# Stick-breaking attention: the sums of later key blocks enter as a high and a low part, and the first values product opens its bank

## The reference, cut to what matters

```
z = einsum('bqhd,bkhd->bhqk', q_b, bk) * HEAD_DIM ** -0.5
causal = kpos[None, :] < qpos[:, None]
log_beta = log_sigmoid(z)
log_one_minus = where(causal, log_sigmoid(-z), 0.0)
tail = cumsum(log_one_minus, reverse=True) - log_one_minus
a = where(causal, exp(log_beta + tail), 0.0)
return einsum('bhqk,bkhd->bqhd', a, bv)
```

## Time and profile before

| | |
|---|---|
| median of 3 runs | 1705.36 us |
| lowest and highest | 1705.3 and 1705.81 us |
| the profiled execution: span from first to last instruction | 1703.1 us |
| its own whole time | not listed apart from the span |
| stick-breaking stage | 955 to 1051 us of the span |

### The profile page before, as it was taken

One profiled execution on the slowest core, in us unless ns is written; L12 is line 12 of the kernel. 1 busy time (PEld: TensorE's weight loads), 2 busy tenths in 40 slices (PEclk: granted clock), 3 DMA queues, 4 the chain that ended last, 5 costly groups with the idle time before them and its releaser, 6 DMA issues.

```text
span 1703.1 us, 23621 instructions
## 1 busy us (share of the span) xinstructions
PE 1694.7 (100%) x8117; PEld 1360.8 (80%) x8117; DVE 877.5 (52%) x1406; ACT 656.0 (39%) x1091; POOL 656.8 (39%) x276
## 2 busy tenths in 40 slices
PE   9999999999999999999999999999999999999998
PEld 7888767788888888888788766778888988888887
DVE  6644875564655551217497675542233775555013
ACT  7333645433222223327524576452223622222122
POOL 2444322344544444435343000224444244444443
PEclk9999999999999999999999999999999999999999
DMA  5345311223333322334322111122333232233231
GB/s 202 118 148 151 102 63 50 75 88 123 99 99 99 98 90 96 99 99 150 114 99 76 50 45 44 50 67 95 99 99 94 88 101 91 97 99 97 101 96 66
DMA packets 47635, 162.29 MB, mean 95 GB/s; under 512 B 5724, under 2 KB 7900, under 8 KB 47304
## 3 DMA queue, kind: packets, MB, share of 16 engines
q1 hardware_dynamic: 43440, 150.70, 27.5%
q10 hardware_dynamic: 4120, 10.59, 1.9%
HBM read 156.91 MB, written 4.76 MB: 95 GB/s over the span
## 4 chain that ended last, share of the span: by engine, by line
PE 52%; issue 32%; POOL 12%; DVE 1%; ACT 1%; DMA 1%; POOLq 0%; SPq 0%; ACTq 0%; DVEq 0%
PE ps L505 14%; PE ps L506 14%; PE ps L507 14%; POOL w_lo L442 12%; PE ps L1131 1%; PE ps L1129 1%; PE ps L1130 1%; PE ps L704 1%; PE ps L686 1%; DMA w_raw<-stream 1%; PE ps L730 1%; PE ps L1030 1%; PE ps L989 1%; PE ps L1011 1%; PE ps L958 1%
## 5 line engine op out<-in xcount | busy, mean ns | idle before, releaser
L442 POOL TENSOR_TENSOR w_lo<-w_raw,w_hi 128x1024 fp32r<-128x1024 f32 x260 | 642.8, 2475 | 1026.2 <-ACT w_hi L1212 999.3
L505 PE MATMUL ps<-u_hi,w_hi 128*128 128x512 f32 x1336 | 539.6, 404 | 0.2 <-ACTq L1802 0.2
L507 PE MATMUL ps<-u_hi,w_lo 128*128 128x512 f32 x1336 | 521.1, 390 | 0.0
L506 PE MATMUL ps<-u_lo,w_hi 128*128 128x512 f32 x1336 | 520.5, 390 | 0.0
L1212 ACT ACTIVATE w_hi<-w_raw 128x1024 fp32r<-128x1024 f32 x271 | 285.4, 1055 | 391.5 <-PE ps L507 326.3
L505 PEld LDWEIGHTS ps<-u_hi,w_hi 128*128 128x128 f32 x1336 | 251.1, 188 | 56.7 <-issue 5.8
L507 PEld LDWEIGHTS ps<-u_hi,w_lo 128*128 128x128 f32 x1336 | 250.8, 188 | 53.4
L506 PEld LDWEIGHTS ps<-u_lo,w_hi 128*128 128x128 f32 x1336 | 251.3, 188 | 50.9 <-issue 1.4
L1635 ACT ACTIVATE tmp<-tmp 128x512 f32<-128x512 f32 x44 | 27.8, 633 | 213.2 <-DVEq L2317 213.2
L2327 DVE TENSOR_TENSOR a_lo<-tmp,a_hi 128x512 f32 (+1 forms) x44 | 104.2, 2368 | 4.7
L505 PE MATMUL ps<-a_hi,w_hi 128*128 (+1 forms) x264 | 102.9, 390 | 0.0
(11 more groups left out here) (410 smaller groups left out, 2434.6 us busy)
## 6 DMA issues: line engine op xcount, KB each, us to landing
w_raw<-stream SPq DMA_DIRECT2D x277, 512.0 KB, 3.5
g_rep<-g_one ACTq DMA_DIRECT2D x1, 2560.0 KB, 12.8
spread<-m_rows ACTq DMA_DIRECT2D x4, 512.0 KB, 4.0
tmp<-tmp ACTq DMA_DIRECT2D x32, 64.0 KB, 2.5
bias<-g_rep ACTq DMA_DIRECT2D x1, 2048.0 KB, 10.1
outT<-hT SPq DMA_DIRECT2D x13, 128.0 KB, 1.8
hT<-xT SPq DMA_DIRECT2D x3, 512.0 KB, 7.5
mem_in<-memT ACTq DMA_DIRECT2D x1, 1024.0 KB, 4.8
```

Of the source, the lines that this page charges most:

```text
L442: pool.tensor_tensor(w_lo[:, slot], w_raw[:, slot], w_hi[:, slot].bitcast(F32), ALU.subtract)\
L505: pe.matmul(out, wh, xh, start=start, stop=False)
L506: pe.matmul(out, wh, xl, start=False, stop=False)
L507: return pe.matmul(out, wl, xh, start=False, stop=stop)
```

## The change

- `negones_r`, a rounded copy of `negones` in its own place, is made by ACT at the start (line 1423 is followed by one more copy).
- The plain fp32 product of line 1011 becomes two fp32r products, `negones_r` times `sums_hi` and times `sums_lo`.
- ACT makes `sums_hi` for both heads of step g-1, at the end of turn g, behind that step's two `sticks`. POOL makes `sums_lo` from it. PE waits for `sums_lo` (`sb_sum_lo`) before the two products.
- The running sums lie in other places: `even_sums` and `odd_sums`. DVE waits, before it overwrites one, until the low part of the sums that lay there has been made.
- The product of zeros goes, with the two memsets on DVE that filled it; the first values product of a pair has `start` set instead.

```diff
+        negones_r = at("negones_r", [P, P], F32R, kept_at + 4 * TAB["negones"])
...
-        sum_tiles = [[tmp[2], tmp[3]], [at("sum2", [P, T], F32, mk_at), at("sum3", [P, T], F32, mk_at + 2 * K)]]
+        sum_at = [arena + 103 * K, mk_at]
+        even_sums = [at(f"even_sums{e}", [P, T - P], F32, sum_at[e]) for e in range(2)]
+        odd_sums = [at(f"odd_sums{e}", [P, T - 2 * P], F32, sum_at[e] + 4 * (T - P)) for e in range(2)]
+        sums_hi = [ar("sums_hi0", [P, T - P], F32R, 72), ar("sums_hi1", [P, T - P], F32R, 78)]
+        sums_lo = [at(f"sums_lo{e}", [P, T - P], F32R, sum_at[e] + 4 * (2 * T - 3 * P)) for e in range(2)]
...
+        def of_sums(h, n):
+
+            return 6 * (h // 2) + 2 * n + h % 2 + 1
...
@@ GpSimd, behind its weight tiles up to BY_VECTOR[0]
+            for h, i in B_STEPS:
+                if i > 0:
+                    n = QT - 1 - i
+                    pool.wait_ge(named("sb_sum_hi"), of_sums(h, n))
+                    pool.tensor_tensor(sums_lo[h % 2][:, 0:T - i * P], sums(h % 2, n, i * P, T),
+                                       sums_hi[h % 2][:, 0:T - i * P].bitcast(F32), ALU.subtract)\
+                        .then_inc(named("sb_sum_lo"), 1)
@@ TensorE
-            pe.wait_ge(named("zeros"), 2)
-            pe.wait_ge(consts, 7)
+            pe.wait_ge(consts, 8)
...
                         if i < QT - 1:
-                            pe.wait_ge(named("sb_acc"), 6 * (h // 2) + 2 * (QT - 2 - i) + e + 1)
-                            m = pe.matmul(ps[:, b, P:w], negones, sums(e, QT - 2 - i, (i + 1) * P, T), start=False,
+                            pe.wait_ge(named("sb_sum_lo"), of_sums(h, QT - 2 - i))
+                            pe.matmul(ps[:, b, P:w], negones_r[:, :], sums_hi[e][:, 0:w - P], start=False,
+                                      stop=False, skip_group_check=True)
+                            m = pe.matmul(ps[:, b, P:w], negones_r[:, :], sums_lo[e][:, 0:w - P], start=False,
                                           stop=True, skip_group_check=True)
...
                     if i == QT - 1:
                         acquire(bo)
-                        pe.matmul(ps[:, bo, :], zero_l[:, :], zero_r[:, :], start=True, stop=False,
-                                  skip_group_check=True)
...
-                                  sticks[(s + e) % 4][:, 0:T - i * P], start=False, stop=e == 1 and i == 0,
+                                  sticks[(s + e) % 4][:, 0:T - i * P], start=i == QT - 1, stop=e == 1 and i == 0,
@@ ScalarE, at the start
             act.activation(negtri_r[:, :], negtri, ACT.Copy).then_inc(consts, 1)
+            act.activation(negones_r[:, :], negones, ACT.Copy).then_inc(consts, 1)
@@ ScalarE, in the stage, behind the two sticks of step g-1
+                    for e in range(2):
+                        h, i = B_STEPS[2 * (g - 1) + e]
+                        if i > 0:
+                            n = QT - 1 - i
+                            act.wait_ge(named("sb_acc"), of_sums(h, n))
+                            act.activation(sums_hi[e][:, 0:T - i * P], sums(e, n, i * P, T), ACT.Copy)\
+                               .then_inc(named("sb_sum_hi"), 1)
@@ VectorE
-            step(dve.memset(zero_l[:, :], 0.0))
-            dve.sem_inc(named("zeros"), 1)
-            step(dve.memset(zero_r[:, :], 0.0))
-            dve.sem_inc(named("zeros"), 1)
...
                         if i > 0:
                             n = QT - 1 - i
+                            if h >= 2 or n == 2:
+                                dve.wait_ge(named("sb_sum_lo"), of_sums(h, n) - (2, 6, 4)[n])
```

More of the change, by code:

```diff
@@ L232, in build @@
         soft_hi = [ar(f"soft_hi{i}", [P, T], F32R, at_kib) for i, at_kib in enumerate((64, 66, 74, 76))]
-        sum_tiles = [[tmp[2], tmp[3]], [at("sum2", [P, T], F32, mk_at), at("sum3", [P, T], F32, mk_at + 2 * K)]]
-        def sums(e, n, c0, c1):
-            x = sum_tiles[e][n % 2]
-            return x[:, c0 - 3 * P:c1 - 3 * P] if n == 0 else x[:, c0:c1]
+        sum_at = [arena + 103 * K, mk_at]
[3 more added lines that the diff above has]
+        sums_lo = [at(f"sums_lo{e}", [P, T - P], F32R, sum_at[e] + 4 * (2 * T - 3 * P)) for e in range(2)]
+        def sums(e, n, c0, c1):
+            first = (QT - 1 - n) * P
+            x = (odd_sums if n % 2 else even_sums)[e]
+            return x[:, c0 - first:c1 - first]
+        def of_sums(h, n):
+            return 6 * (h // 2) + 2 * n + h % 2 + 1
         sticks = [tmp[0], tmp[1], at("stick2", [P, T], F32, mv_at), at("stick3", [P, T], F32, mv_at + 2 * K)]
@@ L257, in build @@
         GATE_BANK = 2
-        zero_l = ar("zero_l", [P, P], BF16, 72)
-        zero_r = ar("zero_r", [P, T], BF16, 73)
         tab_in = ar("tab_in", [P, 2 * P], F32, 96)
@@ L2457, in _ @@
                         j = 2 * g + e
-                        i = B_STEPS[j][1]
+                        h, i = B_STEPS[j]
                         w = T - i * P
```

## The result

The changed kernel takes 1713.9 us (median; 1713.48 to 1714.9) against 1705.49 (1705.3 to 1705.81) for the kernel before on the same chip: ratio 1.005, 95% interval 1.0038 to 1.0062. The profiled execution has a span of 1712.4 us at a granted clock of 0.998.

What follows compares the result with a forecast made beforehand. PE's own order of work was taken as the bound. Lateness at i = 0 of 7.0 us over four pairs, less 0.5 for an earlier S, gave 1705.36 + 6.5 = 1711.9 us; range 1706.0 to 1717.0.

Steps and rivals of the forecast that it cites:

- Off PE, 4.6 us: PE's saving in the stick-breaking stage: 2.5 us at width 384, 1.2 at 256, 0.9 for the zero products.
- PE's own order of work sets the end: In the stick-breaking stage, time taken off PE is won and time PE is made to wait is lost in full.
- The chain from S: From S, a pair's second 384 wide `sticks` start, through ACT, POOL, PE: second head's sums in at S + 4.05.
- Eight waits: PE waiting for POOL's `sums_lo` at the new products' line eight times, longest at width 384 and in the last pair.
- 11 in all: PE's total wait for `sums_lo`, some 11 us, about 2 to 3 us in each pair.
- S itself: Start of the second 384 wide `sticks`: 0 to 0.3 us earlier in each of pairs 2 to 4, -0.5 in all.
- second rival: POOL and DVE hold each other, 0.9 us per pair on the chain: 3.7 us more, 1715.6; 14 in 100.
- The last pair: At i = 0 PE is 2.6 us later, with no next step's z or weight quarter in front of the product.
- three things that the prediction named: POOL much shorter or longer than 1.02 us at 384; waits at i = 1 and 2; clock under 1.00 behind waits.
- A quick POOL: Same chain, but POOL's 384 wide subtraction takes 0.5 us; decides below 0.65: +2.4 us, 1707.8; 16 in 100.
- No wait at i = 0: Low parts are there when PE wants them at width 384, so PE keeps its 4.6 us: 1700.8; 8 in 100.
- The other edits at nothing: DVE's new wait was covered by idle time, the weight tile's high part made early, the extra copy and memsets nothing.

Runs made afterwards that it cites:

- products_alone: Changed kernel without the splitting of the sums on ACT and POOL; the two fp32r products read the step's own softplus parts: 1701.65 us, ratio 0.9978.
- middle_split: Kernel before with the split at width 256 alone, on ACT and POOL as in the change, and no zero product: 1705.64 us, ratio 1.0002.
- middle_on_pool: Kernel before with the split at width 256 alone, both halves on POOL, and no zero product: 1705.48 us, ratio 1.0.
- hi_only: Changed kernel without POOL's subtraction; one product, `negones_r` times `sums_hi`, in place of two: 1706.08 us, ratio 1.0005.
- blanks: Changed kernel with fifteen unread 512 wide bf16 products on PE in the last pair's waits for `soft_lo` and `sums_lo`: 1712.95 us, ratio 1.0044.
- pool_twice: Changed kernel with each low part subtracted twice on POOL, PE waiting for the second: 1732.42 us, ratio 1.016.
- hi_on_pool: Changed kernel with both halves of the split on POOL and no copies for the sums on ACT: 1707.37 us, ratio 1.0013.

## Why the prediction was right, and where by its own steps it was not

The forecast was 1711.9 us; 1713.9 came, by the chain that it named.

- **Off PE, 4.6 us.** The widths cost what was counted: 0.17 us for a 384 wide fp32r product, two of width 256 some 0.23 (0.15 saved was counted, 0.19 would be right). With no sums to wait for, 3.7 us of the sum are won (`products_alone`). "PE's own order of work sets the end" held in full in the pairs 2 and 3, where 1.16 us a pair are won and PE never stands still; in pairs 1 and 4 a second chain, DVE's and ACT's, is close enough behind to keep some 0.5 us each. With POOL at work that chain is 0.5 us later in pairs 2 to 4 (`middle_split`, `middle_on_pool`), for which the sum has no term.
- **The chain from S.** Copies at S + 0.68, as counted; 0.47 each for 0.52; POOL starts at S + 1.28 for 1.34; 0.98 us for 1.02 at width 384. The first head's low part is there at S + 2.27 for 2.36, the second's at S + 3.25 for 3.38. Behind them the hand-over and the weight load were oversized: 0.05 and 0.11 us (the product holds PE for 0.28 instead of 0.17) where 0.14 and 0.19 were counted. The second head's sums are in at S + 3.75 (1030.88 + 0.17) where 4.05 was counted. Eight waits were forecast and four are listed: the first head's wait brings PE to the second head's product just as that one's low part is there (1030.56 and 1030.55), and only the weight load is still waiting. Both heads' chains end together at that point, so no run shows that the first one alone sets the time. 7.0 us of waits for the sums, and 9.7 with the other two kinds, came for "11 in all".
- **S itself.** It was to come some 0.1 to 0.2 us earlier in a pair; it came 0.2 later. From a pair's z of width 256 to the next S, pair 3:

  | | z | S | us |
  |---|---|---|---|
  | before | 1004.75 | 1023.08 | 18.33 |
  | `products_alone`: nothing new on ACT and POOL | 1003.60 | 1021.48 | 17.88 |
  | `hi_only`: ACT's copies, nothing on POOL | 1004.23 | 1022.28 | 18.05 |
  | after | 1008.80 | 1027.30 | 18.50 |

  Pairs 2 and 4 give the same within 0.02. So the work saved on PE does bring S forward, by 0.45; ACT's copies cost 0.17 of it and POOL's work another 0.45, which turns the sign (`hi_only` has one product less on PE, so this split is an estimate). This last is the second rival's mechanism at another place: POOL's 256 wide subtractions run beside DVE's 384 wide one of the second head, ahead of the widest step's z:

```profile
1019.35 0.56 DVE L2489 TENSOR_TENSOR soft_lo<-st,soft_hi 128x384 fp32r<-128x384 f32 x1
...
1020.65 1.07 DVE L2489 TENSOR_TENSOR soft_lo<-st,soft_hi 128x384 fp32r<-128x384 f32 x1
...
1020.57 1.75 POOL L480 TENSOR_TENSOR sums_lo<-odd_sums,sums_hi 128x256 fp32r<-128x256 f32 x2 [4.45 <-ACT sums_hi L1834]
```

  The first head's takes 0.56, the second's 1.07, and the widest step's capped z comes 0.5 us later. ACT waits for it (0.61 us ahead of those exponentials, 0.65 before), so its own copies of width 256 are covered there. The two errors, -0.3 behind S and +0.2 in S against the unmoved one from which 1.6, 1.4 and 1.4 us were worked out, nearly cancel: the first three pairs grew by 1.75, 1.34 and 1.29. That these pairs came out so close is luck in part. The -0.5 taken off the sum for an earlier S did not come.
- **The last pair.** 2.6 us were forecast, 3.98 came. With the clock held up it is 2.50 (`blanks`: 25.73 - 23.23). The missing term is the clock's: 1.48 us in the profiles, 1.0 by the medians, and one of the three things that the prediction named as able to make it wrong. With the -0.5 for S it makes most of the 2.0 us between forecast and median.
- **The rivals.** A quick POOL: 0.98 us at 384, far above the 0.65 from which it would decide, and `pool_twice` confirms the price. POOL and DVE holding each other: real, but some 0.45 us per pair ahead of S (1.8 in all, an estimate from the table above) and none on the chain, where POOL's pairs at 1.96 and 1.97 us have only 128 wide work of DVE beside them; the 3.7 us of the rival were not there, though about half of that was, at the other place. No wait at i = 0: for the sums, `hi_on_pool` reaches it, but at 1705.5 us with the clock held up and not 1700.8, as the waits for bank 0 and for `soft_lo` take over.
- **The other edits at nothing.** DVE's new wait, the weight tile's high part and the extra copy at the start appear in no wait of PE. The first z starts 0.92 us later in the profile of after (956.22 for 955.30) but at 955.57 in that of `blanks`, whose work up to there is the same: it belongs to the execution, not to the change.

## What to carry to other kernels

Before taking work off the busiest engine, find the chain that comes second, and how far behind it is. Here it is DVE's and ACT's work from the widest z to the copy that frees bank 0: left alone it let PE win 1.16 us a pair (`products_alone`); made 0.5 us later by an engine that had been idle, it took most of the saving back (`middle_split`, `middle_on_pool`). An idle engine is not free when it holds up a busy one beside it. A value that was ready early and is sent through two more engines comes as late as the place in the first engine's order at which it is taken up; moving that place forward only helps if what it is moved past has slack. And a wait of a few microseconds on PE can cost more than its length, since the clock can fall behind it, for 1.48 us here.

## What the runs showed of the hardware that was not expected

- **The clock behind short waits.** After 1.43 and 2.44 us without work, 0.7 us apart, the granted clock was 0.54 from 1054.8 to 1058.5, for a loss of 1.48 us; in `hi_only` waits of 1.48 and 1.36 us, 0.6 apart, were followed by 0.50 from 1048 to 1050. Waits of 1.50 to 1.52 in pairs 1 to 3 left the products as they were. Whether one of the two waits would have been enough was not separated. Blank products in the two waits kept the clock at 1.00 in all of five runs.
- **POOL and DVE on SBUF.** The Trainium skill, page "SBUF — State Buffer", section "Who interferes with whom", says that a VectorE operation with two inputs in SBUF contends with a GpSimd operation that reads SBUF. The trace agrees, for a kind of operation that the rows of before didn't show: DVE's 384 wide subtraction 0.56 us alone and 1.07 beside POOL. A copy of DVE's, with one input, is held too: 0.64 us for 0.23 in `middle_on_pool`, where it ends at 1016.28 and POOL's subtraction at 1016.20. POOL's 256 wide subtraction in turn has a mean of 895 ns in after, and 756 in `hi_on_pool`, where DVE's 384 wide one stays at 559.
- **POOL's narrow operations.** In after:

```profile
L480 POOL TENSOR_TENSOR sums_lo<-even_sums,sums_hi 128x384 fp32r<-128x384 f32 x8 | 7.9, 1005 | 25.1 <-ACT sums_hi L1834 25.1
L480 POOL TENSOR_TENSOR sums_lo<-odd_sums,sums_hi 128x256 fp32r<-128x256 f32 x8 | 7.0, 895 | 17.6 <-ACT sums_hi L1834 17.6
L480 POOL TENSOR_TENSOR sums_lo<-even_sums,sums_hi 128x128 fp32r<-128x128 f32 x8 | 3.5, 462 | 45.4 <-ACT sums_hi L1834 45.4
```

  462 ns at 128 columns and 1005 at 384, which is 2.1 ns a column and 0.19 us besides.
